# Experts in 12 passes of 96 + 32 slots, in column groups of 64, 32 and 32, with five experts' weights on chip

## The reference, cut to what matters

```python
s = sigmoid(x @ w_router)                       # 544 x 16
g_idx = argmax over 4 groups of (sum of the two best of s + bias)
e_idx = the two best experts of that group      # 544 x 2
gates = s[e_idx] / sum(s[e_idx])
h = silu(x @ w_gate[e]) * (x @ w_up[e])         # 1024 -> 2 x 256
y = sum over the two e of gate * (h @ w_down[e])  # 256 -> 1024
x = layer_norm(ALPHA * x + y)
```

## Time and profile before

| what | value |
|---|---|
| median of 3 runs | 1448.62 us (1444.24 to 1454.06) |
| span of the profiled execution | 1442.4 us |
| TensorE busy | 1227.5 us, 85% |
| VectorE, ScalarE busy | 660.6 us, 345.5 us |
| expert passes, layer 0 and layer 1 | from 502 to 692 us and from 1202 to 1392 us |
| moved by DMA | 246.34 MB, mean 171 GB/s |

### The profile page before, as it was taken

The page is one execution under the profiler, slowest core; times in us unless marked ns, Lnnn a source line. Parts: engine busy times, 40 slices in busy tenths (PEclk is TensorE's granted clock), DMA queues, the critical chain, the costliest instruction groups (busy, mean ns, idle before and its releaser), DMA issues.

```text
span 1442.4 us, 22134 instructions
## 1 busy us (share of the span) xinstructions
PE 1227.5 (85%) x8330; PEld 772.1 (54%) x8330; DVE 660.6 (46%) x1379; ACT 345.5 (24%) x798; POOL 160.3 (11%) x223
## 2 busy tenths in 40 slices
PE   4989999987898399999599799999699928999950
PEld 2466778973545144454256577799354523444420
DVE  0035798876354301111453369987763351111118
ACT  1044223304321011111142441421332101111110
POOL 0040006104000200000201000350400011000020
PEclk9988999998998599999799699999899958999985
DMA  7087211008614679997512011100473046999943
GB/s 264 8 337 283 73 46 43 7 3 250 228 68 156 236 270 356 366 367 269 199 61 69 25 59 59 45 20 4 149 248 149 5 162 235 357 361 365 365 145 121
DMA packets 68209, 246.34 MB, mean 171 GB/s; under 512 B 8754, under 2 KB 29394, under 8 KB 58706
## 3 DMA queue, kind: packets, MB, share of 16 engines
q1 hardware_dynamic: 49024, 177.17, 34.4%
q0 software_dynamic: 14048, 50.00, 9.6%
q10 hardware_dynamic: 5042, 17.90, 3.0%
HBM read 194.39 MB, written 52.87 MB: 171 GB/s over the span
## 4 chain that ended last, share of the span: by engine, by line
PE 75%; DVE 10%; ACT 4%; DMA 3%; issue 3%; DVEq 2%; SPq 2%; POOL 1%; POOLq 0%; ACTq 0%
PE ps L1249 15%; PE ps L714 13%; PE ps L847 10%; PE ps L1267 8%; PE ps L1210 8%; PE ps L694 7%; PE ps L1240 2%; SPq L451 2%; PE ps L773 1%; PE ps L1082 1%; ACT arena L1320 1%; DMA arena<-in_wa 1%; PE ps L670 1%; DVE arena L1865 1%; DVE arena L2225 1%
## 5 line engine op out<-in xcount | busy, mean ns | idle before, releaser
L1320 ACT ACTIVATE arena<-ps 128x512 f32<-128x512 f32 (+14 forms) x358 | 155.6, 470 | 668.4 <-PE ps L714 157.1
L714 PE MATMUL ps<-arena 128*128 128x272 f32 x1088 | 262.7, 401 | 0.0
L714 PEld LDWEIGHTS ps<-arena 128*128 128x128 f32 x1088 | 210.0, 194 | 51.1 <-issue 5.5
L1249 PE MATMUL ps<-arena 128*128 128x512 f32 x512 | 225.6, 592 | 4.8 <-ACT arena L1320 4.8
L1249 PEld LDWEIGHTS ps<-arena 128*128 128x128 f32 x512 | 96.5, 189 | 127.0 <-issue 127.0
L847 PE MATMUL ps<-arena 64*64 64x64 f32 (+3 forms) x4016 | 149.6, 234 | 12.9 <-DVE arena L2082 10.6
L847 PEld LDWEIGHTS ps<-arena 64*64 64x64 f32 x4016 | 137.0, 136 | 24.6 <-issue 12.7
L694 PE MATMUL ps<-arena 128*128 128x512 f32 (+1 forms) x256 | 107.2, 580 | 22.4 <-DMA arena<-in_wa 19.0
L1267 PE MATMUL ps<-arena 128*128 128x512 f32 x256 | 117.7, 602 | 3.8 <-DVE arena L2535 3.8
L1210 PE MATMUL ps<-arena 128*128 128x512 f32 x256 | 112.4, 594 | 0.0
L2535 DVE COPY arena<-ps 128x256 f32<-128x256 f32 x32 | 13.6, 426 | 188.1 <-PE ps L1256 188.1
(11 more groups left out here) (345 smaller groups left out, 1340.7 us busy)
## 6 DMA issues: line engine op xcount, KB each, us to landing
arena<-in_w_gu SPq DMA_DIRECT2D x32, 2048.0 KB, 9.7
arena<-in_w_dn SPq DMA_DIRECT2D x32, 1024.0 KB, 9.4
arena<-in_wf SPq DMA_DIRECT2D x34, 512.0 KB, 3.3
arena<-rows_in SPq DMA_DIRECT2D x32, 512.0 KB, 9.5
rows_out<-arena ACTq DMA_DIRECT2D x32, 512.0 KB, 8.5
rows_in<-arena POOLq DMA_DIRECT2D x12, 1024.0 KB, 24.0
arena<-in_cache_v POOLq DMA_DIRECT2D x64, 128.0 KB, 5.7
arena<-in_cache_k SPq DMA_DIRECT2D x64, 128.0 KB, 5.7
```

Of the source, the lines that this page charges most:

```text
L714: mm = pe.matmul(ps[:, 2 + 2 * h + n % 2, 0:HALF], m.wf[n % 3][:, c, :], m.xT[:, c, h * HALF:h * HALF + HALF], start=c == 0, stop=c == KC - 1)
L1249: mm = pe.matmul(ps[:, 3 + k, :], m.xgT[:, c, :], m.w_gu[k][:, c, :], start=c == 0, stop=c == KC - 1)
L1320: return act.activation(out, in_, ACT.Copy)
```

## The change

- A pass now has 96 slots of one expert (its own) and 32 slots of another (the shared one). Experts go by fours: experts 0, 1 and 2 of a group have a pass each, and expert 3 of the group has 32 slots in each of the three. 12 passes do what 16 did. An expert with more than 96 rows goes on in one of 12 spare blocks.
- Every matmul of `gate_and_up` and `down` becomes three, on the same input columns, into partitions 0 to 63 and 64 to 95 with the own expert's weights and into 96 to 127 with the shared expert's. A matmul can have 32, 64 or 128 output partitions here, so that 96 are 64 and 32.
- Weights have five places instead of two. Before the passes the weights of the first five experts in the order of use are asked for, the first ones earlier than before; in the passes a place is filled again when the last pass of its expert is through (`REFILL`).
- `row_weights` of the next layer moves from before the passes to the last two of them, because its room is used.
- `dispatch` is written with other steps; the passes of TensorE and SyncE are written out instead of looped; two more blocks of zeros are written to `rows_out` at the start.

The core of the diff:

```diff
+def groups_of(shared, own):
+    return ((slice(0, 64), own), (slice(64, 96), own), (slice(96, P), shared))
...
-            for c in range(KC):
-                mm = pe.matmul(ps[:, 3 + k, :], m.xgT[:, c, :], m.w_gu[k][:, c, :], start=c == 0, stop=c == KC - 1)
+            for c in range(KC):
+                for q, i in groups_of(shared, own):
+                    mm = pe.matmul(ps[q, 3 + k, :], m.xgT[:, c, q], m.w_gu[HOME[i]][:, c, :], start=c == 0, stop=c == KC - 1,
+                                   skip_group_check=True)
...
             for h in range(2):
                 for f in range(2):
-                    mm = pe.matmul(ps[:, 5 + h, :], m.hT[:, f, :], m.w_dn[k][:, f, 512 * h:512 * h + 512],
-                                   start=f == 0, stop=f == 1)
+                    for q, i in groups_of(shared, own):
+                        mm = pe.matmul(ps[q, 5 + h, :], m.hT[:, f, q], m.w_dn[HOME[i]][:, f, 512 * h:512 * h + 512],
+                                       start=f == 0, stop=f == 1, skip_group_check=True)
...
-        up_weights(1, 1)
-        down_weights(1, 1)
+        up_weights(0)
+        down_weights(0)
+        sp.wait_ge(s["rows_stored"], nth(l, "rows_stored", 96))
+        up_weights(1)
+        down_weights(2)
         sp.wait_ge(s["mix_mm"], nth(l, "mix_mm", 5))
-        up_weights(0, 0)
-        down_weights(0, 0)
-        if l + 1 < DEPTH:
-            row_weights(l + 1)
+        down_weights(1)
+        up_weights(2)
+        up_weights(3)
+        down_weights(3)
+        down_weights(4)
+        sp.wait_ge(s["router_mm"], nth(l, "router_mm", 1))
+        up_weights(4)
...
+            if n == PASSES - 1 and l + 1 < DEPTH:
+                sp.wait_ge(s["down_mm"], nth(l, "down_mm", last_pass(13) + 1))
+                sp.wait_ge(s["gu_mm"], nth(l, "gu_mm", last_pass(8) + 1))
+                row_weights(l + 1)
...
-    for n in range(NEXP // 2, BLOCKS // 2):
+    for n in range(PASSES // 2, BLOCKS // 2):
         pool.dma_start(m.rows_out...[:, 2 * n:2 * n + 2, :], m.ln).then_inc(s["zeros_out"], 16)
```

More of the change, by code:

```diff
@@ L45, with last_pass, turn_of @@
 NEXP, DEXP = 16, 256
-BLOCKS = NEXP + 2 * T // P
-SPARE = BLOCKS - NEXP
+CAP = 96
+PASSES = 3 * NEXP // 4
+SPARE = 12
+BLOCKS = PASSES + SPARE
+ORDER = [4 * g + e for g in range(NEXP // 4) for e in (3, 0, 1, 2)]
+HOME = [0, 1, 2, 3, 4, 1, 2, 0, 3, 1, 2, 4, 0, 1, 2, 4]
+def last_pass(i):
+    return 3 * (i // 4) + (2 if i % 4 == 0 else i % 4 - 1)
+def turn_of(i):
+    return HOME[:i].count(HOME[i]) + 1
+def groups_of(shared, own):
+    return ((slice(0, 64), own), (slice(64, 96), own), (slice(96, P), shared))
+REFILL = [[i for i in range(5, NEXP) if max(k for k in range(i) if HOME[k] == HOME[i]) in
+           [k for k in range(NEXP) if last_pass(k) == n]] for n in range(PASSES)]
 ALPHA = (2 * DEPTH) ** 0.25
@@ L75 @@
     ("ones", 1), ("group_order", 4), ("expert_order", 16), ("eps", 2),
+    ("place", 16), ("beyond_cap", 16), ("steps", 4),
 ])
@@ L138, in constants @@
     put("expert_order", np.broadcast_to(16.0 - np.arange(16), (P, 16)))
+    e = np.arange(NEXP)
+    place = np.where(e % 4 == 3, 3 * (e // 4) * P + CAP, (3 * (e // 4) + e % 4) * P)
+    put("place", np.broadcast_to(place + 1, (P, NEXP)))
+    put("beyond_cap", np.broadcast_to(PASSES * P - CAP - place - 2 * CAP * (e % 4 == 3), (P, NEXP)))
+    put("steps", np.broadcast_to(CAP + P * np.arange(4), (P, 4)))
     put("eps", np.broadcast_to(np.array([1e-5, 64e-5], np.float32), (P, 2)))
@@ L330, in memory @@
     m.V = [view(at, 4, NPAGE, WA) for at in (R2 + 4096, R2 + 8192)]
-    m.w_gu = [view(R2 + 6144 * k, KC, 2 * DEXP) for k in range(2)]
-    m.w_dn = [view(R2 + 6144 * k + 4096, 2, DM) for k in range(2)]
+    m.w_gu = [view(at, KC, 2 * DEXP) for at in (R2 + 6144, A0, R2, R1, XT0)]
+    m.w_dn = [view(at, 2, DM) for at in (R2 + 4096, R1 + 6144, R2 + 10240, R1 + 4096, YT0 + 2304)]
     m.xg, m.y = ([view(R4 + at + DM * k, DM) for k in range(2)] for at in (0, 3840))
@@ L342, in memory @@
     m.slot, m.hot_hi, m.hot_lo = (view(YT0 + 352 + 80 * k, 5, NEXP) for k in range(3))
-    m.extra, m.extra_sum, m.shift_to, m.own = (view(YT0 + 592 + NEXP * k, NEXP) for k in range(4))
-    m.beyond, m.count = view(YT0 + 656, 8, NEXP), view(YT0 + 784, 8)
-    m.hi, m.lo, m.gate_hi, m.gate_lo = (view(YT0 + 792 + 5 * k, 5) for k in range(4))
+    m.extra, m.extra_sum, m.shift_to = view(YT0 + 592, NEXP + 1), view(YT0 + 616, NEXP + 1), view(YT0 + 640, NEXP)
+    m.above, m.step = view(YT0 + 656, NEXP, 4), view(YT0 + 720, 5, 4)
+    m.beyond, m.count = view(YT0 + 740, SPARE, NEXP), view(YT0 + 932, SPARE)
+    m.hi, m.lo, m.gate_hi, m.gate_lo = (view(YT0 + 944 + 5 * k, 5) for k in range(4))
     return m
@@ L491, in sync_program @@
             block_rows(k, k, xg_in)
[L492 to L512, removed]
+        for n in range(PASSES):
+            if n + 2 < PASSES:
+                sp.wait_ge(s["xgt_mm"], nth(l, "xgt_mm", n + 1))
+                block_rows(n % 2, n + 2, (s["xg0_in"], s["xg1_in"])[n % 2])
+            if n >= 2 and REFILL[n - 2]:
+                sp.wait_ge(s["down_mm"], nth(l, "down_mm", n - 1))
+                for i in REFILL[n - 2]:
+                    down_weights(i)
+            if REFILL[n]:
+                sp.wait_ge(s["gu_mm"], nth(l, "gu_mm", n + 1))
+                for i in REFILL[n]:
+                    up_weights(i)
+            if n == PASSES - 1 and l + 1 < DEPTH:
+                sp.wait_ge(s["down_mm"], nth(l, "down_mm", last_pass(13) + 1))
+                sp.wait_ge(s["gu_mm"], nth(l, "gu_mm", last_pass(8) + 1))
+                row_weights(l + 1)
         sp.wait_ge(s["planned"], nth(l, "planned", 1))
-        extra = sp.value_load(m.extra_blocks, min_val=0, max_val=BLOCKS - NEXP)
+        extra = sp.value_load(m.extra_blocks, min_val=0, max_val=SPARE)
         with sp.If(extra > 0):
+            sp.wait_ge(s["down_mm"], nth(l, "down_mm", PASSES))
             with sp.Fori(0, SPARE // 2) as e:
@@ L1241, in rows_to_columns, with gate_and_up, down, spare_gate_and_up @@
             mm.then_inc(s["xgt_mm"], 1)
-        def gate_and_up(e, k):
-            pe.wait_ge((s["gu0_in"], s["gu1_in"])[k], nth(l, f"gu{k}_in", e * 16 + 16))
+        def gate_and_up(n):
+            k = n % 2
+            shared, own = 4 * (n // 3), 4 * (n // 3) + 1 + n % 3
+            for i in (shared, own):
+                pe.wait_ge(s[f"gu{HOME[i]}_in"], nth(l, f"gu{HOME[i]}_in", 16 * turn_of(i)))
+            pe.wait_ge(s["h_ready"], nth(l, "h_ready", n - 1))
+            pe.wait_ge(s["xgt_copied"], nth(l, "xgt_copied", n + 1))
+            for c in range(KC):
+                for q, i in groups_of(shared, own):
+                    mm = pe.matmul(ps[q, 3 + k, :], m.xgT[:, c, q], m.w_gu[HOME[i]][:, c, :], start=c == 0, stop=c == KC - 1,
+                                   skip_group_check=True)
+            mm.then_inc(s["gu_mm"], 1)
+        def down(n):
+            pe.wait_ge(s["y_copied_a"], nth(l, "y_copied_a", n))
+            pe.wait_ge(s["y_copied_v"], nth(l, "y_copied_v", n))
+            pe.wait_ge(s["ht_copied"], nth(l, "ht_copied", n + 1))
+            shared, own = 4 * (n // 3), 4 * (n // 3) + 1 + n % 3
+            for i in (shared, own):
+                pe.wait_ge(s[f"dn{HOME[i]}_in"], nth(l, f"dn{HOME[i]}_in", 16 * turn_of(i)))
+            for h in range(2):
+                for f in range(2):
+                    for q, i in groups_of(shared, own):
+                        mm = pe.matmul(ps[q, 5 + h, :], m.hT[:, f, q], m.w_dn[HOME[i]][:, f, 512 * h:512 * h + 512],
+                                       start=f == 0, stop=f == 1, skip_group_check=True)
+            mm.then_inc(s["down_mm"], 1)
+        def spare_gate_and_up(e, k):
+            pe.wait_ge((s["sp0_in"], s["sp1_in"])[k], nth(l, f"sp{k}_in", e * 32 + (32 - 16 * PASSES)))
             pe.wait_ge(s["h_ready"], nth(l, "h_ready", e * 2 + (k - 1)))
@@ L1248, in gate_and_up @@
             for c in range(KC):
-                mm = pe.matmul(ps[:, 3 + k, :], m.xgT[:, c, :], m.w_gu[k][:, c, :], start=c == 0, stop=c == KC - 1)
+                mm = pe.matmul(ps[:, 3 + k, :], m.xgT[:, c, :], m.w_gu[2 * k][:, c, :], start=c == 0, stop=c == KC - 1)
             mm.then_inc(s["gu_mm"], 1)
@@ L1257, in hidden_to_columns, with spare_down @@
             mm.then_inc(s["ht_mm"], 1)
-        def down(e, k):
+        def spare_down(e, k):
             pe.wait_ge(s["y_copied_a"], nth(l, "y_copied_a", e * 2 + k))
@@ L1263, in down @@
             pe.wait_ge(s["ht_copied"], nth(l, "ht_copied", e * 2 + (k + 1)))
-            pe.wait_ge((s["dn0_in"], s["dn1_in"])[k], nth(l, f"dn{k}_in", e * 16 + 16))
             for h in range(2):
                 for f in range(2):
-                    mm = pe.matmul(ps[:, 5 + h, :], m.hT[:, f, :], m.w_dn[k][:, f, 512 * h:512 * h + 512],
+                    mm = pe.matmul(ps[:, 5 + h, :], m.hT[:, f, :], m.w_dn[2 * k][:, f, 512 * h:512 * h + 512],
```

(50 more changed lines are left out.)

70 lines of the change are left out of this document (35 added, 35 removed).

## The result

The changed kernel takes 1681.95 us (median of 4 runs, 1678.9 to 1684.64), the kernel before 1449.2 us beside it. The ratio is 1.1616, with a 95% interval of 1.158 to 1.1653: 16% slower, 233 us. The forecast was 1685 us.

What follows compares the result with a forecast made beforehand. TensorE was taken to set the pace, the DMAs only just keeping it. Passes at 25.24 us add 238.2 us in both layers, `dispatch` saves 2.0: +236 on 1448.6 gives 1685 us, range 1650 to 1720.

Steps and rivals of the forecast that it cites:

- Groups of one width overlap, a change of width doesn't.: Expert matmuls on TensorE: nothing of a new width starts before the old has streamed; each change costs 0.14 to 0.19 us.
- The row that was said to decide: Attention's timeline before: 32 wide groups started 1.12 us after eight 64 wide instructions began, 0.24 after streaming, though sharing no columns.
- A triple at 2.00 us: Three matmuls replacing one in the passes: 4 x 0.43 + 2 x 0.14 = 2.00 us, where one matmul took 0.86.
- The rest of the span: Everything outside the passes: -2.0 us in all, from `dispatch` 1 us shorter in each layer.
- The two groups of 32 run together: Within a triple in the passes, both groups of 32 run beside each other in 2 x 0.43 us.
- rival B: In the passes nothing overlaps, not even the two groups of 32: 2.86 us a triple, 1932 us in all; chance 0.04.
- Weights and queue at zero: Earlier weight loads before the scatter and refills in the passes cost 0; layer 0 passes need 170 GB/s, no refill late.
- `dispatch`, 1 us less: Ahead of the scatter: 10 steps for 15, about 3.4 us for 4.45, a gain of 1 us in each layer.
- First scatter 1 us earlier: Sign expected in the profile after: the first scatter, issued at 484.09 before, comes about 1 us earlier.
- rival C: In the passes the half used array makes the clock fall to its lower level: near 2290 us; chance 0.02.
- Two things run at their limit side by side.: Passes before: TensorE busy 185 of 190 us, DMAs at 0.98 and 361 GB/s; TensorE sets the pace, DMAs only just keep it.
- rival A: Groups of different width overlap: triple 0.86, pass 11.70 us, 1360 us in all, which the DMAs would just allow; chance 0.07.

Runs made afterwards that it cites:

- the sorted version: Changed kernel with, in each block, all matmuls of the group of 64 first, then all of the groups of 32: 1616.39 us.
- the late loads: Weights of fourth and fifth expert asked for only in the passes: 1680.77 us on the changed kernel, 1358.54 us on its version with four groups of 32.

## Why the prediction was right

- *Groups of one width overlap, a change of width doesn't.* Right, and shown by experiment: equal widths give 11.70 us a pass (four 32s, two 64s), mixed widths 25.08, and 25.00 with columns left free between the groups. The row that was said to decide, 355.31 to 356.43 in the earlier trace rows, proved less than the prediction took from it. Its eight instructions are two fours of one width on different columns, and they too ran one behind the other (8 x 0.11 us), against the prediction's own rule for one width. In the program the second four waits for an input of its own (`pt_copied`), which may explain it; a short wait would not show there as idle time, since the modelled ends of 128-column instructions reach past the next start (1.20 us of busy time in 1.12), and the same holds for the start of line 1131 behind them. So the row could not tell a change of width from a group of 64 that runs beside nothing. The run with two groups of 64 could. The forecast's number is the same by either.
- *A triple at 2.00 us.* Measured 1.99. The price of 0.14 for a change was 0.13 in the sorted version. The pass was put at 25.24 and is 25.08; that is 2 us a layer by which the passes were put too high, 3.8 in both. The rest of the span was put at -2.0 us and came out at +0.4 (234.8 - 234.4), so that the two errors partly cancel in the total: the nearness of 1685 to 1682 is in part luck, the pass isn't.
- *The two groups of 32 run together.* They start together at 551.37, so rival B is out.
- *Weights and queue at zero.* 165 GB/s in the passes of layer 0 (170 forecast), no wait of TensorE for weights, none for row weights at the start of layer 1.
- *`dispatch`, 1 us less.* 3.56 us for 4.45, 0.9 less. VectorE's first and last step of it in the timeline after:

```profile
478.81 0.22 DVE L2531 TENSOR_TENSOR arena<-ps,arena 128x64 f32<-128x64 f32 x1 [1.61 <-PE ps L1263]
...
482.20 0.17 DVE L2557 TENSOR_SCALAR ints<-arena 128x5 int32<-128x5 f32 x1
```

- *First scatter 1 us earlier.* Not so in this execution: it is issued at 486.33, 2.2 us later than in the earlier trace rows, although `dispatch` is shorter. 0.8 us were lost before the sample rows of the output projection, which start at 387.98 for 387.14, 1.7 in the output projection, in the stretch shown below, and 0.6 between it and `dispatch`. This is a small term, some 3 us of 233.
- *The clock.* PEclk is 1.00 in the passes: rival C is out.
- *"Two things run at their limit side by side."* Wrong for the DMAs, as the late loads showed: they carried 386 GB/s at 0.95 of their time, more than the 361 at 0.98 in the earlier trace rows. The forecast didn't rest on it; the "just" in rival A did.
- *Rival A* had the right mechanism for one width. Its number, 1360, is what the version with four 32s measures, 1359.

The page "TensorEngine Tiling (Array Packing)" of the Trainium skill, section Key Properties, has the rule that decided: a change of tiling mode drains TensorE, a change of tile does not. Every run here agrees; the price that it leaves out is 0.13 us a change, beside the overlap that is lost.

The version with four groups of 32 beats both kernels: 1359 us, 6.1% under the kernel before. Of the gain of 89 us, 87 are 24 passes of 11.70 us for 32 of 11.49 (368 - 281).

## What to carry to other kernels

Before a matmul is cut into column groups, look in the trace for the distance of starts where groups of different width follow each other; if the second waits for the first, cut into groups of one width, even if that makes more instructions. When widths have to differ, sort by width: that saves the changes, though not the lost overlap. Busy time doesn't show a half used array; the time of a block per pass does.

## What the hardware showed that was not expected

In three of the nine profiles of this study the granted clock fell to its lower level for 3.4 us in the output projection of layer 0, while TensorE was busy. Windows after the change, and below them before (0.95 and 0.71 are 0.5 and 2.9 us at half the clock):

```profile
435.00:440.00 5.00, 5.00 (x39) 3.25 (x38) 2.72 (x4) 0.11 (x1) 0.00 (x0) 0.95 0.00 0
440.00:445.00 5.00, 5.00 (x10) 2.21 (x9) 0.98 (x2) 0.18 (x1) 0.00 (x0) 0.71 0.00 0
```

```profile
440.00:445.00 5.00, 5.00 (x13) 2.17 (x12) 0.43 (x1) 0.00 (x0) 0.00 (x0) 1.00 0.00 0
```

Ahead of it TensorE had done the router's 32 short instructions (16 columns each, 2.50 us from 436.88). The 16 instructions of the output projection behind them took 8.66 us for 6.88 of the next 16, and for 6.96 of the same 16 before. The chain after, and below it before:

```profile
436.88 2.50 PE ps L1223 x32
439.38 8.66 PE ps L1244 x16
...
448.91 6.88 PE ps L1244 x16
```

```profile
438.54 6.96 PE ps L1210 x16
```

Six profiles with the same work there show no such fall; why it comes in some and not in others stays open.

The DMAs carried 386 GB/s for 140 us beside a TensorE that never stood still for weights; 361 in the steady part of the kernel before was its demand, 4 MB a pass, and not their limit. A DMA share of 0.98 was no sign that no more could be carried.
